# Two fused blocks on one core: the first two column blocks of two feed-forwards are multiplied row by row together, the second's weights split between the rows of the layer norm

## The reference

```python
x = _layer_norm(DN_ALPHA * x + h, ln_attn_g[layer], ln_attn_b[layer])
f = _conv_ffn(x, ffn_w_in[layer], ffn_conv_w[layer], ffn_conv_b[layer], ffn_w_out[layer])
...
def _conv_ffn(x, w_in, conv_w, conv_b, w_out):        # w_in: 1024 x 5632
    u = x @ w_in
    up = jnp.pad(u, ((0, 0), (CONV_WIDTH - 1, 0), (0, 0)))
    u = sum(conv_w[j] * up[:, j:j + s] for j in range(CONV_WIDTH)) + conv_b
    g, val = u[..., :D_FF], u[..., D_FF:]               # D_FF = 2816
    return (jax.nn.silu(g) * val) @ w_out
```

## Time and profile before

| what | value |
|---|---|
| median of 3 runs | 2325.05 us (2325.0 to 2325.57) |
| profiled execution, its own time | 2309.08 us |
| its span | 2307.3 us |
| TensorE busy | 2174.2 us (94%) |
| DVE busy | 1158.7 us (50%) |
| ACT busy | 1003.6 us (43%) |
| POOL busy | 943.9 us (41%) |

### The profile page before, as it was taken

How to read it: one execution, slowest core, us unless ns; L and a number is a source line. 1 busy time by engine, 2 the same in 40 slices (tenths; PEclk the granted TensorE clock), 3 DMA queues, 4 the chain that set the end, 5 groups by cost and what they waited for, 6 DMA issues and landing times.

```text
span 2307.3 us, 27947 instructions
## 1 busy us (share of the span) xinstructions
PE 2174.2 (94%) x10712; PEld 1806.9 (78%) x10720; DVE 1158.7 (50%) x1852; ACT 1003.6 (43%) x2027; POOL 943.9 (41%) x714
## 2 busy tenths in 40 slices
PE   7999899999998898799999999799999999999997
PEld 6788778888877777678888878687677887888886
DVE  3445565554343666465554354775764326444322
ACT  5656444443225555244443245666543234333221
POOL 3655553443356663353443342322413344232232
PEclk9999999999989999899999998999999998999998
DMA  4111123222222221123222211111112231322221
GB/s 160 55 56 58 53 93 108 92 92 103 101 71 83 92 73 46 37 78 106 92 93 102 101 62 66 37 37 37 37 65 74 101 110 55 110 92 98 97 101 53
DMA packets 29844, 183.06 MB, mean 79 GB/s; under 512 B 3984, under 2 KB 4112, under 8 KB 11920
## 3 DMA queue, kind: packets, MB, share of 16 engines
q1 hardware_dynamic: 29712, 181.27, 22.8%
HBM read 174.97 MB, written 2.10 MB: 77 GB/s over the span
## 4 chain that ended last, share of the span: by engine, by line
PE 82%; DVE 7%; ACT 4%; issue 3%; POOL 2%; DMA 1%; SPq 0%; POOLq 0%; DVEq 0%; ACTq 0%
PE PS L1457 80%; PE PS L1582 1%; POOL LO L2746 1%; DVE bQS L2197 1%; PE PS L1695 1%; ACT HI L1781 0%; DVE XL L2274 0%; DMA RAW<-wall 0%; DVE aQS L2197 0%; ACT cEM L2156 0%; DVE LO L2197 0%; DVE cCVT L2624 0%; DVE YH L2299 0%; PE PS L1630 0%; DVE T_f L2269 0%
## 5 line engine op out<-in xcount | busy, mean ns | idle before, releaser
L2746 POOL TENSOR_TENSOR LO<-RAW,HI 128x512 fp32r<-128x512 f32 (+2 forms) x382 | 541.5, 1433 | 618.7 <-ACT HI L1781 618.7
L1457 PE MATMUL PS<-XH,HI 128*128 128x512 f32 (+1 forms) x1584 | 638.0, 403 | 25.0 <-DVE XL L2197 6.9
L1457 PE MATMUL PS<-XH,LO 128*128 128x512 f32 (+1 forms) x1584 | 625.5, 395 | 0.0
L1457 PE MATMUL PS<-XL,HI 128*128 128x512 f32 (+1 forms) x1584 | 619.9, 396 | 1.6 <-DVE XL L2274 1.5
L1781 ACT ACTIVATE HI<-RAW 128x512 fp32r<-128x512 f32 (+3 forms) x668 | 366.0, 607 | 171.4 <-PE PS L1457 168.0
L2197 DVE TENSOR_TENSOR LO<-RAW,HI 128x512 fp32r<-128x512 f32 (+2 forms) x286 | 305.3, 1072 | 246.3 <-ACT HI L1781 246.0
L1457 PEld LDWEIGHTS PS<-XH,HI 128*128 128x128 f32 (+1 forms) x1584 | 302.4, 191 | 88.4 <-issue 21.3
L1457 PEld LDWEIGHTS PS<-XH,LO 128*128 128x128 f32 (+1 forms) x1584 | 301.8, 191 | 65.5 <-issue 0.9
L1457 PEld LDWEIGHTS PS<-XL,HI 128*128 128x128 f32 (+1 forms) x1584 | 300.8, 190 | 64.4 <-DVE XL L2274 4.1
L1457 PE MATMUL PS<-HL,HI 128*128 128x512 f32 x528 | 205.7, 389 | 0.0
L1457 PE MATMUL PS<-HH,HI 128*128 128x512 f32 x528 | 205.7, 389 | 0.0
(11 more groups left out here) (404 smaller groups left out, 3314.4 us busy)
## 6 DMA issues: line engine op xcount, KB each, us to landing
RAW<-wall SPq DMA_DIRECT2D x138, 1024.0 KB, 4.8
RAW<-wall SPq DMA_DIRECT2D x24, 896.0 KB, 4.5
bROT<-bTQ SPq DMA_DIRECT2D x64, 64.0 KB, 2.0
RAW<-wall SPq DMA_DIRECT2D x5, 512.0 KB, 3.3
XF<-xT SPq DMA_DIRECT2D x4, 512.0 KB, 5.4
outT<-XR SPq DMA_DIRECT2D x8, 256.0 KB, 2.0
FP<-cfp SPq DMA_DIRECT2D x1, 1024.0 KB, 6.8
MKF<-cmask SPq DMA_DIRECT2D x1, 704.0 KB, 11.0
```

Of the source, the lines that this page charges most:

```text
L1457: return e.matmul(out, a, b, start=start, stop=stop)
L2746: return e.tensor_tensor(out, x, h.bitcast(F32), ALU.subtract)
```

## The change

The diff does three things, for the norms "a0" and "a1" and the feed-forwards "0" and "1" only.

1. The split of B begins in the norm: its four parts are put between the rows of the norm (`second = split_steps(...)`, one piece ahead of each of the first `ln` steps), where before they were put between the matmuls of A.
2. A and B are multiplied together by the new `lin_two`: row 0 of A, row 0 of B, row 1 of A, row 1 of B, and so on, 12 matmuls for each row of X. Their two evacuations (`ue`) both follow after the last row.
3. C's and D's copies to HI wait for the end of the two rows of A or B whose place they take (`part_end`), no longer for the whole unit.

```diff
@@ -453,7 +453,7 @@
-        due[0], due[1] = (split_steps(i + 1), 2.0) if i + 1 < len(sequence) else (None, 0)
+        due[0], due[1] = (split_steps(i + 1), 2.0) if i + 1 < len(sequence) and i + 1 not in split_early else (None, 0)
@@ -522,6 +522,26 @@
+    def lin_two(keys, src):
+
+        banks, t0 = [pick() for _ in range(4)], len(tiles)
+        for n, key in enumerate(keys):
+            i = take(key)
+            made = [(i, k) for k in range(places[key][1])]
+            for j in range(2):
+                tiles.append(Tile(made, 128 * j, 128, banks[2 * n + j], src))
+        for kk in range(len(made)):
+            for t in (t0, t0 + 2):
+                if kk % 2:
+                    i = tiles[t].parts[kk][0]
+                    for T in tiles[t:t + 2]:
+                        T.incs.add(kk)
+                    ag.part_end[i, kk // 2] = ("lin", ("m2", t, kk))
+                step_of_two(t, kk)
+                tick()
+                tick()
+        return [(t0, t0 + 1), (t0 + 2, t0 + 3)]
+
@@ -587,7 +607,15 @@
         for j in range(2, 8):
             put("lnm", n, j)
+        second = None
+        if n in ("a0", "a1"):
+            for _ in due[0]:
+                pass
+            second = split_steps(len(order) + 1)
+            split_early.add(len(order) + 1)
         for j in range(9):
+            if second is not None:
+                next(second, None)
             if j < 8:
                 s = put("ln", n, j)
@@ -735,7 +763,12 @@
-            waiting.append((j,) + tuple(lin_fm(("up" + lay, j), "X", together=(j == 0))))
+            if lay != "2" and j == 0:
+                pair = lin_two([("up" + lay, 0), ("up" + lay, 1)], "X")
+            if lay != "2" and j < 2:
+                waiting.append((j,) + pair[j])
+            else:
+                waiting.append((j,) + tuple(lin_fm(("up" + lay, j), "X", together=(j == 0))))
@@ -1775,8 +1808,10 @@
-                    if i >= 2:
+                    if i >= 2 and (i - 2, 0) not in ag.part_end:
                         e.wait_ge(*when_(ag.unit_end[i - 2]))
+                if (i - 2, p) in ag.part_end:
+                    e.wait_ge(*when_(ag.part_end[i - 2, p]))
```

More of the change, by code:

```diff
@@ L257, in __init__ @@
         self.steps, self.tiles, self.order, self.bank_of, self.free_of = [], [], [], {}, {}
-        self.unit_end, self.count, self.tile_of, self.high_of = {}, {}, {}, {}
+        self.unit_end, self.part_end, self.count, self.tile_of, self.high_of = {}, {}, {}, {}, {}
     def number(self):
@@ L377, in agenda @@
     chores, together_chores = [], []
-    seen = set()
+    seen, split_early = set(), set()
     def put(*step):
```

## The result

The changed kernel is slower: 2333.13 us median of 20 runs (2322.67 to 2340.57) against 2321.92 us for the kernel before in 20 runs of its own. The ratio is 1.0057 with a 95% interval of 1.0044 to 1.0069, or +13.2 us (+10.2 to +16.0) on the median of before; the two medians themselves lie 11.2 us apart. The forecast was +11.2 us. The profiled execution took 2328.66 us, its span 2326.9 us. Ratios are of fast runs alone, and one execution of the kernel before that took 9040.79 us is therefore left out of the ratio in experiment 9.

The account below looks back on a forecast made before the run. TensorE was taken to bound the kernel. Waits in rows -0.6, XL row 0 +3.4, clock in norms +1.3, D late +5.4, clock behind it +1.7 sum to +11.2 us: 2325.05 becomes 2336.3, range 2329.5 to 2341.5.

Parts of the forecast that it names:

- XL row 0: In each norm, B's inserted LO part 0 delays XL row 0 on DVE; 1.7 us each, +3.4 in the sum.
- D late: With T the end of A and B, D starts at T + 13.6; TensorE waits 2.7 us per feed-forward, 5.4 in all.
- The rival by which the evacuations overlap: A's and B's evacuations overlap, so D isn't late and only the norm pays: +4.1 us, 2329.2; chance 0.10.
- 1.7, by the row of the same form: Inserted subtraction on DVE in each norm: 1.7 us, from the row of same place and form; bounds 0.7 and 2.3.
- the estimate of 2.3 us for an insertion: By the port-lock rule alone, DVE's insertion costs one POOL instruction (1.63) plus its own 0.69; the sum 1.2 us higher.
- Clock in the norms +1.3: TensorE's low clock lasts longer behind the wait for XL row 0: 1 us in a0, 0.3 in a1.
- waits in the rows -0.6: More matmuls per row remove TensorE's waits from row 1 on: -0.5 us in the first feed-forward, -0.1 in the second.
- Clock behind D, one of the two, +1.7: The clock falls behind one of the two gaps at D, losing 1.7 us; bounds 0 and 3.4.
- a number of fixed waits: The 16 us between the profiled execution of before and the timed median is fixed, so the median becomes 2336.3.
- A smaller misreading: In the norm, ACT is idle for more than half the time, so its copies for B's split cost nothing.

Follow-up runs that it names:

- experiment 9: experiment 7's kernel with XL row 0 put ahead of the second row's subtraction on DVE in the two norms; ratio to before 0.9996 (0.9979 to 1.0013).
- experiment 1: The changed kernel with D's split put between A's evacuation and B's; ratio to before 1.0046 (1.0029 to 1.0062).
- experiment 6: The changed kernel without the release by parts, so C's copies wait for all of A; one trace, no ratio, D 1.7 and 1.95 us later behind the pair.
- experiment 2: The changed kernel with part 0 of B's split put into the statistics and part 2 behind XL row 2; ratio to before 1.0046 (1.0029 to 1.0062).
- experiment 4: The changed kernel with B's split still in the norm's rows but A multiplied alone and B behind it; ratio to before 1.005 (1.0031 to 1.0069).
- experiment 5: The changed kernel with parts 0 and 2 of B's LO both ahead of the norm's second row; one trace, no ratio, XH to XL 5.86 and 5.87 us.
- experiment 3: The changed kernel with the edits of experiment 1 and experiment 2 together; ratio to before 1.0002 (0.9988 to 1.0016).
- experiment 7: experiment 3's kernel with E's split put ahead of C's evacuation too; ratio to before 1.0002 (0.9985 to 1.0018).

## Why the prediction was right, point by point

**The sum.** From two traces each of before and after, per feed-forward, as means of four. From the first XH matmul to the first XL: 2.09 us before, 3.94 after, +1.85. From there to C's first: 22.29 and 23.37, +1.08. From C's to D's first: 10.88 and 13.68, +2.80. From D's to F's: +0.1. Together 5.8 us, so 11.7 us for both, within the interval of the timed runs (10.2 to 16.0). The forecast, by the same division, was 1.7, 0.35, 2.7 and 0.85: 5.6. So two terms, XL row 0 and D late, were right in mechanism and size; that the total was so near is partly luck, as the two after them show.

**D late.** Forecast at T + 13.6, measured at T + 13.68 in a0, with ACT's operations within 0.07 us of the forecast ones. Experiments 1 and 6 show that ACT's queue makes it: the gap goes when D's copies go ahead of the second evacuation, and grows by 1.2 when the queue starts later. The rival by which the evacuations overlap fell: the second starts 0.54 us behind the first's HH. The Trainium skill, TensorE: Matmul & The Clock Gate, section "Architectural detail: the array is 16× 32×32, not 1× 128×128", by which ACT's queue is strictly first in, first out, agrees with that row.

**XL row 0.** Forecast +1.7 us, measured +1.85 in the mean; experiments 2, 4 and 5 (none, alone, double) show that it is DVE's insertion. The step "1.7, by the row of the same form" hid a point. The inserted subtraction took 0.74 us in one norm of the changed kernel and 1.76 or 1.77 in the three others, but that is not yet its price: behind the short one, the subtraction of row 1 took 1.76 us. In the second trace of the kernel before, the same subtraction had been the short one, in norm a0:

```profile
310.38 0.81 DVE L2261 TENSOR_TENSOR T_a<-MS_a,YH 128x512 f32<-128x512 f32 x1
```

Which one is short goes with how DVE's operations meet POOL's rows. In the norms where POOL's first subtraction began 2.8 us ahead of the first XH matmul, the distance from XH to XL is 2.51 and 2.53 us before and 4.2 in the three after; where it began 2.5 to 2.6 us ahead, it is 1.57 in the one norm before and 3.17 in the one after. Like against like, an insertion costs 1.6 to 1.7 us, whichever of the two operations is the short one, and the second insertion of experiment 5 cost 1.7 again. Unlike norms set against each other mislead: in a1 of the two first traces the distances are 1.74 (POOL began 2.3 us ahead) and 4.20 (2.8 ahead). The Trainium skill, SBUF — State Buffer, section "Who interferes with whom", has the port pair that DVE and GpSimd share as an exclusive lock. The traces agree in that DVE's subtraction takes up to 1.77 us against POOL's rows and 0.69 alone; the estimate of 2.3 us for an insertion, worked out in the prediction from that rule, is more than like norms show.

**Two terms were mis-sized and made up for each other.** "Clock in the norms +1.3, waits in the rows -0.6" came out as +2.2 together and not +0.7. The waits in the rows were hardly there to be won: from A's row 2 on, the 36 matmuls took 8.62 us in the one norm that the 0.5 us came from, but 8.18 to 8.22 in the three others, where 8.16 is the pace without waits. And the low clock behind XL row 0 lasted longer than I took from a1: why, stays open (below). "Clock behind D, one of the two, +1.7" was 0: it fell in none of the four gaps in the traces of the change. One error of 1.5 us too little stood beside one of 1.7 too much.

**The base.** The prediction took the 16 us between the profiled execution of before and the median for "a number of fixed waits". No run shows such waits: 2309.08 us lies within the scatter of that kernel's 20 timed runs (2306.95 to 2326.12), and their median is 2321.92 and not 2325.05. So the forecast of the profiled execution, 2320.3, was 8.4 us under the 2328.66 measured, and that of the median, 2336.3, was 3.2 us over. A smaller misreading changed no term: in the earlier trace rows ACT is busy 8.54 of 16 us, so it isn't idle for more than half of them.

**What the trace as a whole would have misled to.** The profiled spans differ by 19.6 us, the two stretches account for 11.3 of it. Of the rest, 5.0 us lie between D of the first feed-forward and the second norm (656.6 us before, 661.6 after), and the second trace of before has 660.6 there. That isn't the change.

**Left open.** In experiments 2, 3 and 7, with XL row 0 early again, the way from the first XL matmul to C is still some 0.7 us longer than before (mean 22.94 of six against 22.29 of four). Row 0 of B runs wholly at the low clock in four of the six. Whether the interleaved order brings the clock back later, or four norms happened to fall badly, isn't settled. In the other two (a1 of experiments 3 and 7) the pace of the high clock is back from the twelfth matmul on, as in three of the four norms of before, and the way is 22.43 and 22.37 us against 22.35 to 22.43 there, so the order costs nothing where the clock is the same. The length of the wait ahead of XL row 0 doesn't explain it alone: with the longest waits, in experiment 5, the way is 22.98 and 22.41 us, and in experiment 9, with none, 21.9 and 22.2.

## What to carry to other kernels

Before work is put between the rows of a stage, look at which row the waiting engine stands at: here all the excess lay ahead of row 0, the added work stood ahead of just that row, and more matmuls per row had nothing to win. When two units are merged, their evacuations come due together, and what stood between them in the queue (here D's copies) comes a whole evacuation later, here 6.4 us of ACT's queue, of which 2.8 us reached TensorE: sum the queue of the evacuating engine from the merged end to the next due time. Work for later goes where the engine idles (here the statistics). The merged order itself was no longer behind only once row 0 was made first, and by less than the times can show.

## What the runs showed of the hardware

A gap of 2.6 us in a stream of matmuls was followed by a lower granted clock in some cases and not in others. The windows give the stretch, its length, busy time of PE, PEld, DVE, ACT and POOL, and then the granted clock, here 1.00 and 0.77 (part of the stretch at 1.2 GHz). Behind D's gap in experiment 2, both feed-forwards:

```profile
349.80:355.80 6.00, 5.97 (x26) 4.98 (x27) 4.25 (x5) 2.60 (x5) 3.53 (x3) 1.00 0.36 109
1048.50:1054.50 6.00, 6.00 (x21) 4.82 (x22) 4.23 (x5) 2.58 (x5) 3.51 (x3) 0.77 0.39 117
```

And behind the gaps of 3.8 us in experiment 6:

```profile
358.00:364.00 6.00, 6.00 (x20) 4.79 (x20) 4.25 (x5) 2.55 (x5) 3.51 (x3) 0.72 0.32 116
1062.00:1068.00 6.00, 6.00 (x20) 4.79 (x21) 4.24 (x5) 2.55 (x5) 3.51 (x3) 0.72 0.39 115
```

Of eight gaps of 2.6 us (the two traces of the change, experiments 2 and 5) two were followed by the low level, at 0.77 and 0.72 over 6 us, a loss of 1.4 and 1.7 us; both of the gaps of 3.8 us were. And one and the same DVE subtraction against POOL's rows, the inserted one, took 0.74 us in one norm and 1.64 to 1.77 in the nine others with one insertion. Two traces of one kernel differ by 0.94 us in the distance from XH to XL of the same norm (2.51 against 1.57), so one trace isn't enough to price a wait there.
